# First mixer of a two-block transformer kernel: the gates' causal mask is added in PSUM, the exponentials read PSUM directly, and one projection tile and two convolutions change place

## The reference, cut to what matters

```python
qkv = silu(causal_dwconv(h @ w_in[:, :4096], conv_w))     # q, k, v; four taps
g = -exp(a_log) * softplus(a + dt_bias)                   # one log gate per token and head
gc = cumsum(g)                                            # within a block of 128 tokens here
D[i, j] = exp(gc[j] - gc[i]) if i <= j else 0             # the decays, 128 x 128 per block and head
keys    = -(k k^T) * D * beta / |k|^2                     # what the inverse is made from
queries =  (k q^T) * D
```

## Time and profile before

| | |
|---|---|
| runs | 1355.17, 1358.7, 1359.31 us; median 1358.7 |
| profiled execution, its own time | 1357.43 us |
| its span, first to last instruction | 1355.6 us |
| mean granted TensorE clock | 0.997 |
| PE busy | 1331.9 us (98%) |
| DVE busy | 878.3 us (65%) |
| ACT busy | 714.3 us (53%) |
| POOL busy | 181.7 us (13%), nearly all before 256 us |

### The profile page before, as it was taken

How to read it: one execution, slowest core, us unless ns; L and a number is a source line. 1 busy time by engine, 2 the same in 40 slices (tenths; PEclk the granted TensorE clock), 3 DMA queues, 4 the chain that set the end, 5 groups by cost and what they waited for, 6 DMA issues and landing times.

```text
span 1355.6 us, 18763 instructions
## 1 busy us (share of the span) xinstructions
PE 1331.9 (98%) x7209; PEld 1132.7 (84%) x7209; DVE 878.3 (65%) x1434; ACT 714.3 (53%) x1181; POOL 181.7 (13%) x327
## 2 busy tenths in 40 slices
PE   9998999999999999999999999999999999999998
PEld 8898898878888898888888887888888877888887
DVE  7886877576555476565554798775554687755553
ACT  7775465445444365454453566564444566544541
POOL 1387878400020000000000000000000000000000
PEclk9999999999999999999999999999999999999999
DMA  8756554356665555266656464166655432666552
GB/s 249 196 158 162 134 141 131 107 161 205 186 185 185 168 166 168 70 216 181 186 185 193 137 213 142 55 199 183 197 176 190 152 123 63 191 197 186 188 186 79
DMA packets 171060, 223.24 MB, mean 165 GB/s; under 512 B 11650, under 2 KB 137403, under 8 KB 170971
## 3 DMA queue, kind: packets, MB, share of 16 engines
q1 hardware_dynamic: 166976, 213.03, 50.7%
q0 software_dynamic: 2224, 7.03, 2.2%
q10 hardware_dynamic: 1770, 1.99, 0.5%
HBM read 217.67 MB, written 4.33 MB: 164 GB/s over the span
## 4 chain that ended last, share of the span: by engine, by line
PE 79%; DVE 12%; ACT 3%; DMA 2%; issue 2%; POOL 1%; SPq 0%; ACTq 0%; DVEq 0%; POOLq 0%
PE psum L982 23%; PE psum L984 22%; PE psum L983 22%; DVE w_low L729 3%; PE psum L1213 2%; PE psum L1219 2%; PE psum L1482 2%; PE psum L1515 1%; PE psum L1438 1%; DMA ring<-in_gdn_w_in 1%; PE psum L973 1%; ACT w_high L715 1%; DVE work L901 1%; DVE arena L2813 1%; PE psum L1501 1%
## 5 line engine op out<-in xcount | busy, mean ns | idle before, releaser
L729 DVE TENSOR_TENSOR w_low<-ring,w_high 128x1024 fp32r<-128x1024 f32 (+3 forms) x395 | 478.5, 1219 | 329.1 <-ACT w_high L715 327.4
L715 ACT ACTIVATE w_high<-ring 128x1024 fp32r<-128x1024 f32 (+3 forms) x395 | 410.7, 1048 | 428.0 <-PE psum L984 414.2
L982 PE MATMUL psum<-w_high,hT 128*128 128x512 f32 (+2 forms) x944 | 368.8, 391 | 0.0
L984 PE MATMUL psum<-w_high,hT 128*128 128x512 f32 (+2 forms) x944 | 365.9, 388 | 0.0
L983 PE MATMUL psum<-w_low,hT 128*128 128x512 f32 (+2 forms) x944 | 365.6, 387 | 0.0
L982 PE MATMUL psum<-w_high,parts 128*128 128x512 f32 (+1 forms) x532 | 209.3, 393 | 1.2 <-DVE parts L2821 1.1
L984 PEld LDWEIGHTS psum<-w_high,hT 128*128 128x128 f32 x944 | 177.3, 188 | 35.9
L984 PE MATMUL psum<-w_high,parts 128*128 128x512 f32 (+1 forms) x532 | 206.3, 388 | 0.0
L983 PEld LDWEIGHTS psum<-w_low,hT 128*128 128x128 f32 x944 | 177.5, 188 | 34.3
L982 PEld LDWEIGHTS psum<-w_high,hT 128*128 128x128 f32 x944 | 177.4, 188 | 34.4
L983 PE MATMUL psum<-w_low,parts 128*128 128x512 f32 (+1 forms) x532 | 206.1, 387 | 0.0
(11 more groups left out here) (305 smaller groups left out, 1366.6 us busy)
## 6 DMA issues: line engine op xcount, KB each, us to landing
ring<-in_ffn_w_gate_up SPq DMA_DIRECT2D x176, 256.0 KB, 3.3
ring<-in_w_gate_up SPq DMA_DIRECT2D x176, 256.0 KB, 3.2
ring<-in_gdn_w_in SPq DMA_DIRECT2D x48, 512.0 KB, 4.6
ring<-in_ffn_w_down SPq DMA_DIRECT2D x44, 512.0 KB, 3.2
ring<-in_w_down SPq DMA_DIRECT2D x44, 512.0 KB, 3.2
ring<-in_da_w_qkv SPq DMA_DIRECT2D x24, 512.0 KB, 4.5
ring<-in_gdn_w_out SPq DMA_DIRECT2D x16, 512.0 KB, 3.4
ring<-in_mla_w_out SPq DMA_DIRECT2D x8, 512.0 KB, 3.9
```

The lines of the kernel that those rows point to most:

```text
L715: nc.scalar.activation(piece_slot(w_high, n), piece_slot(ring, n), ACT.Copy).then_inc(s.w_hi, 1)
L729: nc.vector.tensor_tensor(piece_slot(w_low, n), piece_slot(ring, n), piece_slot(w_high, n).bitcast(F32), ALU.subtract).then_inc(s.w_lo, 1)
L982: mm(out, lhs[0], rhs[0], start=start, stop=False)
L984: return mm(out, lhs[1], rhs[0], start=False, stop=stop)
```

## The change

The mask of the gates becomes a bf16 tile `shade_gates` (0 where i <= j, -1e38 elsewhere), made by POOL early, in the place of `shade_window`, which is now made only when all gate rows are done. `gate_rows` adds it with one product per bank (identity, bf16, 512 columns with the shade repeated for four heads). The eight Relu, the long Exp and the DVE product become eight Exp straight from PSUM with bias -gc[i], which signal `d_ready`. DVE makes -gc beside gc. Tile 9 goes to bank 0. Convolution 8 moves ahead of `split_low` of piece 14 and of `query_products(0)`; convolution 9 moves ahead of `split_low` of piece 15. Cut to its core:

```diff
         def tile_bank(i):
-            return B[(6, 7, 5, 3, 7, 6, 0)[i] if i < 7 else 6 + i % 2][:, 0:SEQ]
+            return B[(6, 7, 5, 3, 7, 6, 0, 7, 6, 0)[i] if i < 10 else 6 + i % 2][:, 0:SEQ]
...
                     if i == 6:
-                        pe.wait_ge(s.diff_ready, 1)
+                        pe.wait_ge(s.d_ready, 1)
                     elif i >= 4:
-                        pe.wait_ge(s.conv_done, {4: 2, 5: 2, 7: 5, 8: 6}.get(i, i - 1))
+                        pe.wait_ge(s.conv_done, {4: 2, 5: 2, 7: 5, 8: 6, 9: 7, 11: 8}.get(i, i - 1))
...
                 if r == 0 and g == 0:
+                    pe.wait_ge(s.conv_done, 10)
                     pe.wait_ge(s.mask_ready, 1)
...
+                else:
+                    pe.wait_ge(s.gate_shade, 1)
                 for t in range(T):
                     for h in range(GH):
-                        last = mm(B[...][:, h * P:(h + 1) * P], gl[...].to_broadcast([P, P]), const("cum"), start=True, stop=True)
+                        mm(B[...][:, h * P:(h + 1) * P], gl[...].to_broadcast([P, P]), const("cum"), start=(h == 0), stop=False, ...)
+                    last = mm(by_head(B[...][:, :]), ident_b, shade_gates.unsqueeze(1).to_broadcast([P, GH, P]),
+                              start=False, stop=True, skip_group_check=True)
...
             def key_products(g):
                 if g:
-                    pe.wait_ge(s.diff_ready, g + 1)
+                    pe.wait_ge(s.d_ready, g + 1)
...
-            def gate_diff(g):
+            def gate_exp(g):
...
-                        last = f(g_p[:, t, h, :], B[...], ACT.Relu, scale=-1.0, bias=gcum[:, t, n:n + 1])
-                last.then_inc(s.diff_ready, 1)
-            def gate_exp(g):
-                act.wait_ge(s.diff_ready, g + 1)
-                f(both(g_p), both(g_p), ACT.Exp, scale=-1.0).then_inc(s.dexp_ready, 1)
+                        last = f(g_p[:, t, h, :], B[...], ACT.Exp, bias=minus_gcum[:, t, n:n + 1])
+                last.then_inc(s.d_ready, 1)
...
-            def gate_causal(g):
-                dve.wait_ge(s.dexp_ready, g + 1)
-                tt(both(g_p), both(g_p), const("incl")..., ALU.mult).then_inc(s.d_ready, 1)
...
             own(v.tensor_copy(gcum..., B[4][:, 0:T * VH]))
+            own(ts(minus_gcum..., B[4][:, 0:T * VH], -1.0, None, ALU.mult))
...
             split_low(dve, tile_piece[6] + SPLIT)
+            conv(8)
             split_low(dve, tile_piece[7] + SPLIT)
             query_products(0)
...
-            tiles(8)
-            tiles(9)
+            conv(9)
+            split_low(dve, tile_piece[8] + SPLIT)
+            split_low(dve, tile_piece[9] + SPLIT)
...
(POOL, behind its first six DMA issues)
+            pool.wait_ge(s.rows_loaded, 16 * 3)
+            pool.wait_ge(s.gates_loaded, 32)
+            own(ts(block_step[:, 0:P], const("incl"), -1.0, 1e38, ALU.add, ALU.mult))
+            copy(ident_b, ident)
+            own.wait()
+            copy(shade_gates, block_step[:, 0:P]).then_inc(s.gate_shade, 1)
...
(POOL, behind the angles)
-            pool.wait_ge(s.rows_loaded, 16 * 3)
+            pool.wait_ge(s.gb_psum, GROUPS)
             pool.wait_ge(s.late_loaded, 48)
-            copy(ident_b, ident)
```

More of the change, by code:

```diff
@@ L167, in __init__ @@
         self.gb_psum = sem("gb_psum")
-        self.diff_ready = sem("diff_ready")
-        self.dexp_ready = sem("dexp_ready")
+        self.gate_shade = sem("gate_shade")
         self.d_ready = sem("d_ready")
@@ L325, in program @@
         ident_b, shade_mla, shade_causal, shade_window = (shades[:, n * P:(n + 1) * P] for n in range(4))
+        shade_gates = shade_window
         rope = sb("rope", 2 * 2 * T * 32)[:, :].rearrange("p (b f t n) -> p b f t n", b=2, f=2, t=T)
@@ L551, in program @@
         gl = cell(T * VH).rearrange("p (t n) -> p t n", t=T)
-        gcum = cell(T * VH).rearrange("p (t n) -> p t n", t=T)
+        gcum, minus_gcum = (cell(T * VH).rearrange("p (t n) -> p t n", t=T) for _ in range(2))
         ed0 = cell(VH)
@@ L1151, in gate_rows @@
                     pe.wait_ge(s.kq_sq, 2 * g + (2 if g == 1 else 1))
+                else:
+                    pe.wait_ge(s.gate_shade, 1)
                 for t in range(T):
                     for h in range(GH):
-                        last = mm(B[(4 if g else 0) + t][:, h * P:(h + 1) * P],
-                                  gl[:, t, g * GH + h:g * GH + h + 1].to_broadcast([P, P]), const("cum"), start=True, stop=True)
+                        mm(B[(4 if g else 0) + t][:, h * P:(h + 1) * P],
+                           gl[:, t, g * GH + h:g * GH + h + 1].to_broadcast([P, P]), const("cum"), start=(h == 0), stop=False,
+                           skip_group_check=True)
+                    last = mm(by_head(B[(4 if g else 0) + t][:, :]), ident_b, shade_gates.unsqueeze(1).to_broadcast([P, GH, P]),
+                              start=False, stop=True, skip_group_check=True)
                 last.then_inc(s.gb_psum, 1)
@@ L1999, in gate_diff @@
                         n = g * GH + h
-                        last = f(g_p[:, t, h, :], B[(4 if g else 0) + t][:, h * P:(h + 1) * P], ACT.Relu, scale=-1.0,
-                                 bias=gcum[:, t, n:n + 1])
-                last.then_inc(s.diff_ready, 1)
-            def gate_exp(g):
-                act.wait_ge(s.diff_ready, g + 1)
-                f(both(g_p), both(g_p), ACT.Exp, scale=-1.0).then_inc(s.dexp_ready, 1)
+                        last = f(g_p[:, t, h, :], B[(4 if g else 0) + t][:, h * P:(h + 1) * P], ACT.Exp,
+                                 bias=minus_gcum[:, t, n:n + 1])
+                last.then_inc(s.d_ready, 1)
             def copy_v(g):
@@ L2074, in _ @@
             act.wait_ge(s.gcum_ready, 1)
-            gate_diff(0)
             gate_exp(0)
@@ L2122, in _ @@
             z_pieces(0, 1)
-            gate_diff(1)
             gate_exp(1)
@@ L2146, in _ @@
             copy_images(0)
-            gate_diff(2)
             gate_exp(2)
@@ L2174, in _ @@
             split_high(act, tile_piece[27] + SPLIT)
-            gate_diff(3)
             gate_exp(3)
@@ L2771, in beta_of @@
                 return beta_k[g][:, t * GH:(t + 1) * GH]
-            def gate_causal(g):
-                dve.wait_ge(s.dexp_ready, g + 1)
-                tt(both(g_p), both(g_p), const("incl").unsqueeze(1).to_broadcast([P, T * GH, P]), ALU.mult).then_inc(s.d_ready, 1)
             def key_products(g):
@@ L2852, in _ @@
             own(v.tensor_copy(gcum.rearrange("p t n -> p (t n)"), B[4][:, 0:T * VH]))
+            own(ts(minus_gcum.rearrange("p t n -> p (t n)"), B[4][:, 0:T * VH], -1.0, None, ALU.mult))
             own.wait()
@@ L2858, in _ @@
             split_low(dve, tile_piece[2] + SPLIT)
-            gate_causal(0)
             conv(4)
@@ L2887, in keys_made @@
             def keys_made(g):
-                gate_causal(g)
                 key_scales(g)
@@ L2965, in _ @@
             split_low(dve, tile_piece[19] + SPLIT)
-            gate_causal(2)
             first_added(0)
@@ L2994, in _ @@
             key_scales(3)
-            gate_causal(3)
             first_added(1)
```

## The result

The changed kernel takes 1351.53 us, median of 6 runs (1350.02 to 1352.49), beside 1358.99 for the kernel before, 6 runs (1355.17 to 1360.31): ratio 0.995, 95% interval 0.994 to 0.996. It is 7.5 us faster where 2.1 were forecast. The time lies inside the range by 0.2 us only, and is that of the first rival. The two profiled executions, from which the readings of these two kernels come, took 1357.43 us before and 1351.1 after, 6.3 us apart.

What follows compares the result with a forecast made beforehand. POOL's chain to the image load, ending 3.79 us after TensorE's line, was taken to decide: -3.0 + 0.92 for late shades = -2.1 us, from 1357.43 to 1355.3 us; range 1351.3 to 1358.8.

Steps and rivals of the forecast that it cites:

- the first rival: POOL's chain to the image load: more comes off, restart moves 4 to 6.6 us, half clock goes; 1350.1 to 1353.4; chance 0.24.
- What bounds the kernel: Up to 115 us: TensorE's line and the ACT, DVE, POOL, store, load chain compete; the second ends last by 3.79 us.
- Part 1: Gates of group 0 on ACT and DVE: tap 4 about 0.97 us earlier, convolution 4 and key products 1.54 earlier.
- Part 2: TensorE up to tile 10: tile 9's 2.17 us wait goes; tile 10 starts 3.3 us earlier, about 0.8 of wait left.
- Part 3: Eight added shade products on TensorE at 0.23 us each; groups 0 and 1 hidden in waits, groups 2 and 3 paid.
- The 0.92: Cost in us of the shades of groups 2 and 3 on TensorE behind 115 us, beside nothing.
- the second rival: Image wait: images land no earlier, late shades cost 0.46 to 1.8 us; 1357.9 to 1359.3; chance 0.15.
- Part 4: POOL's chain, the deciding term: 1.54 + 1.49 = 3.0 us earlier, TensorE's restart at the images from 115.00 to 112.0.
- Everything on POOL behind it: POOL after the store of group 1's keys moves uniformly by 3.0 us, image load from 106.58 to 103.6.
- I take these two as equal: POOL stalls beside DVE: group 1's mask going gains 0.85 us, meeting the low split of piece 15 loses 0.85.
- The gap stays, and so does the half clock: TensorE before the first images: arrives at 108.4, waits 3.6 us until 112.0, half clock behind it.
- The wait at the last images: Rival at group 3's image load: TensorE, 2.1 us earlier, waits 1.7 there; about 1357.0; chance 0.11.

Runs made afterwards that it cites:

- New gates in groups 0 and 1 only: Changed kernel with gates of groups 2 and 3 made as before (Relu, long Exp, DVE mask, no shade): 1351.68 us, ratio 0.9964 to the kernel before.
- POOL late: Changed kernel with twelve small memsets on POOL ahead of the first images' store: 1354.23 us, ratio 0.9966 to the kernel before.
- the fourth experiment: Changed kernel with IMAGES_STEP 6 for 3, so POOL fetches the second images three steps later: 1351.36 us, ratio 0.9943 to the kernel before.
- the last experiment: Changed kernel without the bank and convolution moves, ACT's squares of group 1's keys ahead of the SiLU of pair 5: 1351.53 us, ratio 0.9962.
- group 1 only: Changed kernel with the new gates in group 1 alone, groups 0, 2 and 3 as before: 1353.52 us, ratio 0.9975 to the kernel before.
- the moves alone: Kernel before with only tile 9's bank, its waits and convolutions 8 and 9 moved: 1357.9 us, ratio 0.9996.
- exponential back: Changed kernel with eight Relu and one long Exp back on ACT in all groups, shade kept, no DVE mask: 1357.1 us, ratio 0.9995.

## Why the prediction was right and wrong

The range held by its edge. The term that was said to decide came out at twice its size, and two things that were forecast with it, the gap and the half clock, were gone. That the time still fell inside is luck: the range had been drawn wide enough to take in most of the first rival.

**What bounds the kernel: right.** Two chains compete for 115 us and POOL's ended last. Moving TensorE's alone gave nothing, delaying POOL's alone cost 3.5 us.

**Part 1: right.** Tap 4 at 35.17 (35.28 foretold), convolution 4 at 35.73 (35.77), key products 1.57 us earlier (1.54), eight Exp 2.18 (2.15).

**Part 2: right up to tile 10, short behind it.** Tile 10 at 52.34 (52.0) with 0.82 of wait (0.8), full clock. Missed: the squares of group 1 stand on ACT behind a SiLU that waits for convolution 11, and TensorE, being 3 us earlier, waits 1.76 at 66.18. It arrives at the images at 110.44 and not at 108.4. The moves bring nothing in the end.

**Part 3: the price right, the placing half right.** 0.21 us a shade, against 0.23. But those of group 2 are not "beside nothing": a wait for the image copies takes them. Those of group 3 stand in TensorE's line and cost 0.44 where they can be compared ("New gates in groups 0 and 1 only", 172.97 against 173.41). The 0.92 should have been about 0.44; what is left of that at the end no run shows. (The lower bound of 0.06 a shade would give 0.24 for four, not the 0.46 that the second rival uses.)

**Part 4, the step that failed: the 3.0 us of POOL's chain measured 5.9.** Up to the store of the keys the working held (82.28, foretold 82.5). Behind it I let "Everything on POOL behind it" move by 3.0. It moved by 2.70 more: 1.33 from blocked instructions, above all the last product (1.70 to 0.65), 1.37 from the store of the images, whose landing the DMA view gives as 5.3 us before and 3.9 after. The 1.70 I had named, in the rival alone; the store's landing I had not looked at. "I take these two as equal" traded one mask for one split. Up to the store of the keys that came out: eight of POOL's instructions take over 1.1 us in either trace. Behind it there are six before and four after, so the chain met a different set of splits there. The coincidences above (1.70 to 1.73 us beside low splits, 0.65 beside none) agree with the exclusive lock of the Trainium skill, page "SBUF — State Buffer", section "SBUF: two separate sides". What an edit gains by it is not told by counting the edit's own instructions.

**"The gap stays, and so does the half clock": wrong.** The load lands at 100.67 + 8.3 = 108.97, TensorE comes at 110.44. The 4.56 us gained at the images are the gap of 3.79 and 0.77 of earlier arrival. The half clock's end was not worth the 1.6 us that the rival added: from the images to the products 36.8 us on (151.84 before, 147.31 after), the two traces keep 4.5 us between them. At full clock TensorE runs into two shades (0.43) and waits of 0.30 and 0.23 for ACT and DVE, 0.96 in all; no trace with a half clock at this place has those two waits. Where the rest went was not followed up. "POOL late" gives the half clock's price with the shades in place: 0.5 to 0.6. The rival's 1350.1 to 1353.4 held in part for another reason: 1.62 came at the second images, 1.38 of it the wait that I had said would slide along. How much of that lasted is open, as a like wait in the fourth experiment cost some 0.6 at the end.

**The other rivals.** Images landing no earlier did not happen. The wait at the last images did not come in the change (244.59, no wait), and did come, 1.37 us, with the new gates in group 0 alone.

## What to carry to other kernels

When a chain on a second engine is about to move, read its instructions one by one against the engine that blocks it, and every store's landing with it: a uniform shift is the one outcome that did not occur. When a wait at a meeting point is less than what a plausible shift could remove, work out both sides of that point, since the gain stops where the other chain arrives. Test a two-part edit by its halves: here the halves were worth 2.0 us and nothing that could be told, and the whole 7.1. When a half is put back, put its semaphores back as well: here a rebuilt wait cost 0.57 us and hid what the shades of group 3 are worth.

## What the runs showed of the hardware that was not expected

- In these traces a table load did not wait with the instruction that it serves. For group 1 the changed kernel's gate rows end with a shade product at 71.41, and ACT's timeline has the load before that, with the Exp directly behind:

```profile
70.75 1.28 ACT L2006 ACT_TABLE_LOAD   x1
72.04 2.18 ACT L2006 ACTIVATE work<-psum,small 128x128 f32<-128x128 f32 x8
```

I had assumed this in Part 4; here it is seen. Before, the load stood between Relu and Exp and could not be early.

- The length of a wait does not tell the clock behind it. After 2.17 us before tile 9 it was half, after 2.01 in "POOL late" it was 0.50; after 2.10 at 54.73 in the last experiment it was full. In "group 1 only" waits of 1.17 and 0.82, two microseconds apart, were followed by 0.56, and 1.18 and 0.82 in "the moves alone" by 1.00. (Windows: 54 to 57 us in "group 1 only" and "the moves alone", 54.73 to 57.7 in the last experiment.) What decides was not settled.
- The store of the images (128 KB) landed in 3.6 to 4.4 us in the nine traces whose gates of group 1 are wholly new ("POOL late" and "group 1 only" among them), and in 5.2 to 6.1 in the five that have the mask or the long Exp in group 1. It was not faster for an idler queue: while it was under way the DMA engines moved 247 GB/s in the change (96.45 to 100.4 us) and 246 before (101.0 to 106.3). Nor does being earlier explain it: "POOL late" stores at 100.22 and takes 4.2, "exponential back" at 99.26 and takes 6.1. What does was not tested; the order among the weight loads would be a guess.
